# Attention with values of two pairs of heads in buffers, and the output products as two column tiles

## The reference

```python
s_win = jnp.einsum('brqhd,brwkhd->bhrqwk', qg, k_strip).astype(jnp.float32) * scale
s_win = jnp.where(col_mask[:, None, :], s_win + bias.astype(jnp.float32), NEG_INF)
s_ctx = jnp.einsum('brqhd,bchd->bhrqc', qg, k_ctx).astype(jnp.float32) * scale
s = jnp.concatenate([s_win.reshape(B, NA_HEADS, rows, GRID_W, n_win), s_ctx], axis=-1)
p = jax.nn.softmax(s, axis=-1).astype(v.dtype)
o = (jnp.einsum('bhrqwk,brwkhd->brqhd', p_win, v_strip)
     + jnp.einsum('bhrqc,bchd->brqhd', p_ctx, v_ctx))
```

## Time and profile before

| what | value |
|---|---|
| median of 3 runs | 4186.23 us (4182.61 to 4192.26) |
| profiled execution: span, the only time that the page gives of it | 4189.2 us |
| PE busy over the span | 92% |
| PEld busy | 83% |
| DVE busy | 63% |
| ACT busy | 32% |
| POOL busy | 14% |

### The profile page before, as it was taken

The page is one execution under the profiler, slowest core; times in us unless marked ns, Lnnn a source line. Parts: engine busy times, 40 slices in busy tenths (PEclk is TensorE's granted clock), DMA queues, the critical chain, the costliest instruction groups (busy, mean ns, idle before and its releaser), DMA issues. The chain is left out here.

```text
span 4189.2 us, 60711 instructions
## 1 busy us (share of the span) xinstructions
PE 3859.8 (92%) x21534; PEld 3457.5 (83%) x21534; DVE 2630.6 (63%) x5384; ACT 1359.1 (32%) x1748; POOL 594.4 (14%) x516
## 2 busy tenths in 40 slices
PE   7989999878849969799999999999979999999999
PEld 6878777656538759688888888888869999999999
DVE  1313344346553358757786877777767777788887
ACT  1113333335541131123343424242423333333332
POOL 0000000000000000022222232323212222222221
PEclk7779999999979979899999999999989999999999
DMA  4411111111133311256777685958699999999997
GB/s 172 157 60 52 53 52 40 34 46 40 48 107 107 108 63 40 78 193 210 230 239 256 211 286 181 308 168 301 191 311 357 345 345 348 330 389 346 347 346 274
DMA packets 373028, 813.75 MB, mean 194 GB/s; under 512 B 30704, under 2 KB 207600, under 8 KB 369520
## 3 DMA queue, kind: packets, MB, share of 16 engines
q1 hardware_dynamic: 299120, 542.84, 37.6%
q0 software_dynamic: 73728, 268.47, 18.7%
HBM read 681.69 MB, written 129.50 MB: 194 GB/s over the span
## 5 line engine op out<-in xcount | busy, mean ns | idle before, releaser
L85 PE MATMUL s_ps_a<-back_dense_hi,s_u_hi 128*128 128x512 f32 (+1 forms) x2048 | 715.0, 349 | 47.2 <-DVE s_u_lo L1500 31.9
L85 PE MATMUL c_ps_y<-c_wa_hi,c_v_hi 128*128 128x384 f32 x2048 | 686.6, 335 | 30.1 <-DVE c_wa_lo L1832 30.1
L86 PE MATMUL s_ps_a<-back_dense_lo,s_u_hi 128*128 128x512 f32 (+1 forms) x2048 | 697.6, 341 | 0.0
L87 PE MATMUL s_ps_a<-back_dense_hi,s_u_lo 128*128 128x512 f32 (+1 forms) x2048 | 693.7, 339 | 0.0
L86 PE MATMUL c_ps_y<-c_wa_lo,c_v_hi 128*128 128x384 f32 x2048 | 685.2, 335 | 0.0
L87 PE MATMUL c_ps_y<-c_wa_hi,c_v_lo 128*128 128x384 f32 x2048 | 685.1, 335 | 0.0
L1812 ACT ACTIVATE c_v_hi<-c_v_raw 128x1024 fp32r<-128x1024 f32 x256 | 271.7, 1061 | 657.9 <-PE c_ps_y L87 616.5
L1440 POOL DMA_INDIRECT s_row<-in_u_rows,back_expert x128 | 159.3, 1245 | 2266.4 <-DVE back_expert L1602 1823.7
L85 PEld LDWEIGHTS s_ps_a<-back_dense_hi,s_u_hi 128*128 128x128 f32 x2048 | 391.3, 191 | 96.1 <-DVE s_u_lo L1500 33.3
L1830 DVE TENSOR_TENSOR c_v_lo<-c_v_raw,c_v_hi 128x1024 fp32r<-128x1024 f32 x256 | 313.6, 1225 | 195.4 <-ACT c_v_hi L1812 179.8
L87 PEld LDWEIGHTS s_ps_a<-back_dense_hi,s_u_lo 128*128 128x128 f32 x2048 | 388.7, 190 | 46.8
(11 more groups left out here) (317 smaller groups left out, 7018.3 us busy)
## 6 DMA issues: line engine op xcount, KB each, us to landing
c_v_raw<-in_v SPq DMA_DIRECT2D x256, 512.0 KB
s_u_raw<-in_u SPq DMA_DIRECT2D x130, 512.0 KB
act_scratch<-s_a SPq DMA_DIRECT2D x128, 384.0 KB
gm_scratch<-s_gm SPq DMA_DIRECT2D x48, 1024.0 KB
c_a<-act_scratch SPq DMA_DIRECT2D x256, 192.0 KB
c_g<-gm_scratch SPq DMA_DIRECT2D x256, 192.0 KB
a_w<-in_w_ada SPq DMA_DIRECT2D x16, 1024.0 KB, 4.7
q_raw<-in_w_pq SPq DMA_DIRECT2D x17, 512.0 KB, 3.6
```

Of the source, the lines that this page charges most:

```text
L85: nc.tensor.matmul(out, w_hi, x_hi, start=first, stop=False)
L86: nc.tensor.matmul(out, w_hi, x_lo, start=False, stop=False)
L87: return nc.tensor.matmul(out, w_lo, x_hi, start=False, stop=last)
```

## The change

Three edits. The value tiles get a second buffer, with a semaphore for each; the values of pair h + 1 are issued in turn 2 of pair h, behind the store of the finished pair and the slab, after the last output products of pair h - 1. The output products are split by head: 64 value columns of the head as weights, the 64 query columns of the head as moving operand, written to that head's 64 partitions of `ps_o`, which is now 64 columns wide; the products of the two heads alternate. DVE copies `ps_o` with one instruction.

```diff
-        v = m.sb("v", [P, VT, P])
-        v_odd = m.sb("v_odd", [P, VS, P])
+        v = m.sb("v", [P, 2, VT, P])
+        v_odd = m.sb("v_odd", [P, 2, VS, P])
...
-        ps_o = ps_t[:, ALL:ALL + P]
+        ps_o = ps_t[:, ALL:ALL + HD]
...
-                if h >= 1:
-                    sp.wait_ge(o_ready, ROWS * h)
-                sp.dma_start(v[:], io["v_scr"][:, cols].rearrange("(j p) c -> p j c", p=P)).then_inc(v_in, 16)
+                if h >= 2:
+                    sp.wait_ge(o_ready, ROWS * (h - 1))
+                sp.dma_start(v[:, h % 2], io["v_scr"][:, cols].rearrange("(j p) c -> p j c", p=P)).then_inc(v_in[h % 2], 16)
...
                     if h >= 1:
-                        values_in(h)
                         sp.wait_ge(o_copied, ROWS * h)
                         sp.dma_start(io["oa_scr"][h - 1], o[:, (h - 1) % 2]).then_inc(o_stored, 16)
                     if h + 1 < PAIRS:
                         slab_load(h + 1)
+                        values_in(h + 1)
...
-                    nc.vector.tensor_copy(o[0:HD, r // ROWS % 2, cols], ps_o[0:HD, 0:HD])
-                    nc.vector.tensor_copy(o[HD:P, r // ROWS % 2, cols], ps_o[HD:P, HD:P]).then_inc(o_copied, 1)
+                    nc.vector.tensor_copy(o[:, r // ROWS % 2, cols], ps_o).then_inc(o_copied, 1)
...
                     if r % ROWS == 0:
-                        pe.wait_ge(v_in, 32 * (r // ROWS + 1))
+                        pe.wait_ge(v_in[r // ROWS % 2], 32 * (r // ROWS // 2 + 1))
...
                     for j in range(NT):
-                        v_tile = tiles[:, first // 2 + j] if j < KEYS // P else v[:, T // P + j - KEYS // P]
-                        last = nc.tensor.matmul(ps_o, v_tile, p_t[:, r % 2, j], start=(j == 0), stop=(j == NT - 1))
+                        v_tile = tiles[:, first // 2 + j] if j < KEYS // P else own[:, T // P + j - KEYS // P]
+                        for head in (slice(0, HD), slice(HD, P)):
+                            last = nc.tensor.matmul(ps_o[head], v_tile[:, head], p_t[:, r % 2, j, head], start=(j == 0), stop=(j == NT - 1))
```

More of the change, by code:

```diff
@@ L411, in attention_and_gates @@
         ps_p = m.ps("ps_p", [P, 2, HALF])
-        ps_o = ps_t[:, ALL:ALL + P]
-        consts_in, slab_in, v_in, hi_done, lo_done, piece_ready, consts, rstd_done, slab_done, s_ready, row_max, row_stat = (
-            m.cleared_sem(x, sems) for x in ("consts_in", "slab_in", "v_in", "hi_done", "lo_done", "piece_ready", "consts", "rstd_done", "slab_done",
+        ps_o = ps_t[:, ALL:ALL + HD]
+        consts_in, slab_in, hi_done, lo_done, piece_ready, consts, rstd_done, slab_done, s_ready, row_max, row_stat = (
+            m.cleared_sem(x, sems) for x in ("consts_in", "slab_in", "hi_done", "lo_done", "piece_ready", "consts", "rstd_done", "slab_done",
                                              "s_ready", "row_max", "row_stat"))
@@ L417, in attention_and_gates @@
             m.cleared_sem(x, sems) for x in ("exp_done", "p_norm", "p_ready", "t_ready", "t_copied", "o_ready", "o_copied", "o_stored"))
-        raw_in, piece_used, gate_stored = ([m.cleared_sem(f"{x}{b}", sems) for b in range(2)] for x in ("raw_in", "piece_used", "gate_stored"))
+        raw_in, piece_used, gate_stored, v_in = ([m.cleared_sem(f"{x}{b}", sems) for b in range(2)] for x in ("raw_in", "piece_used", "gate_stored", "v_in"))
         block = ctx.enter_context(nc.Block())
@@ L444, in values_in @@
                 cols = slice(h * P, (h + 1) * P)
-                if h >= 1:
-                    sp.wait_ge(o_ready, ROWS * h)
-                sp.dma_start(v[:], io["v_scr"][:, cols].rearrange("(j p) c -> p j c", p=P)).then_inc(v_in, 16)
-                sp.dma_start(v_odd[:], io["v_scr"][GRID_W:GRID_W + VS * P, cols].rearrange("(j p) c -> p j c", p=P)).then_inc(v_in, 16)
+                if h >= 2:
+                    sp.wait_ge(o_ready, ROWS * (h - 1))
+                sp.dma_start(v[:, h % 2], io["v_scr"][:, cols].rearrange("(j p) c -> p j c", p=P)).then_inc(v_in[h % 2], 16)
+                sp.dma_start(v_odd[:, h % 2], io["v_scr"][GRID_W:GRID_W + VS * P, cols].rearrange("(j p) c -> p j c", p=P)).then_inc(v_in[h % 2], 16)
             def slab_load(h):
@@ L694, in _ @@
                     if r % ROWS == 0:
-                        pe.wait_ge(v_in, 32 * (r // ROWS + 1))
+                        pe.wait_ge(v_in[r // ROWS % 2], 32 * (r // ROWS // 2 + 1))
                     pe.wait_ge(t_copied, r + 1)
                     first = row0[r % ROWS]
-                    tiles = v if first % 2 == 0 else v_odd
+                    own, odd = v[:, r // ROWS % 2], v_odd[:, r // ROWS % 2]
+                    tiles = own if first % 2 == 0 else odd
                     for j in range(NT):
-                        v_tile = tiles[:, first // 2 + j] if j < KEYS // P else v[:, T // P + j - KEYS // P]
-                        last = nc.tensor.matmul(ps_o, v_tile, p_t[:, r % 2, j], start=(j == 0), stop=(j == NT - 1))
+                        v_tile = tiles[:, first // 2 + j] if j < KEYS // P else own[:, T // P + j - KEYS // P]
+                        for head in (slice(0, HD), slice(HD, P)):
+                            last = nc.tensor.matmul(ps_o[head], v_tile[:, head], p_t[:, r % 2, j, head], start=(j == 0), stop=(j == NT - 1))
                     last.then_inc(o_ready, 1)
```

## The result

The changed kernel takes 4140.49 us (median of 4 runs, 4136.62 to 4145.12) against 4187.42 of the kernel before in the same job; the ratio is 0.9889, 95% interval 0.9875 to 0.9903. A second job gave 0.9886 (0.9868 to 0.9905). So it is faster by 47 us, where 21 were forecast: the sign was right and the size less than half of it.

The account below looks back on a forecast made before the run. The prediction took PE to bound the kernel in the attention; its terms, -24.4 + 3.6 - 0.6 = -21.4 us, gave 4164.8 us against the median of 4186.23, with a range from 4120 to 4212.

Parts of the forecast that it names:

- The values' wait: PE's three waits for values in the attention would go with the slower turns they cause: -24.4 us, bounds 18.2 and 24.4.
- The output products: 24 small pairs a turn at 58 ns, 1.39 us against 1.34, over 64 turns: +3.6 us.
- the lower end: Output products of the two heads wholly side by side: 12 x 58 = 0.70 us a turn, -41 us.
- the signs: Changed profile: two heads' records starting together; turns with a projection piece longer than about 9.1 us or shorter than 8.5.
- The switch: PE going between whole-array and half-array products and back, twice a turn: taken as nothing.
- the upper end: Full emptying of PE at each change between whole and half array: 0.27 us, twice a turn, 64 turns, +34 us.
- Rival 3: Heads' output products side by side, with full emptying at each change of array use: 4154 us, chance 0.18.
- DVE's copy: Two copies of the outputs become one, saving time only in the stage's last three rows: 3 x 0.2 = -0.6 us.
- Clock: Shorter output products would not bring PE's clock down; at worst another 1.4 us in some turns.
- the forecast: Whole program 21.4 us faster, 4164.8 us, own range 4158 to 4178, chance 0.38.
- rivals 2 and 3: Heads' output products side by side: switches free, 4120 us, chance 0.12; or with full switches, 4154 us, chance 0.18.
- a third of 4: Rival 4: values' wait returns as another wait, 5 to 24 us of gain lost, 4170 to 4189 us, chance 0.06.

Follow-up runs that it names:

- the first experiment: Values in two buffers and loaded a pair ahead, output products and the two copies as before, against the kernel before the change: 4162.37 us, ratio 0.9936.

## Why the prediction was wrong

**The values' wait, 24.4 us: right.** With that edit alone the stage's distances sum to 24.3 us less. SP's new order delayed nothing.

**The output products, +3.6 us: wrong, and this is the step that failed.** The prediction put it so: "I take half, 53.3 ns", with 4.7 ns on top, and 24 of them in a row. The price was right: 0.058 us for a pair on its half, in both orders. "In a row" was not. With the halves alternating the two heads' pairs run side by side, and the products take 12 x 58 = 0.70 us, the lower end that the text itself worked out. So a term of +3.6 us stands where -41 for the products and at most 21 for the switches belong; the tiles alone took 24.8 us off the 61 distances (1.7 of it the clock) and 2.3 off the last rows. The choice went to the value "nearest to the rows", but every row was of products over the whole array: they bear on the price of a pair and say nothing on concurrency. The prediction had named the signs, and two were met: two records of the two heads starting together (0.007 us apart), and a turn with a piece shorter than 8.5 us (8.47).

**The switch, 0: wrong too, the other way.** 0.33 us there and back, about 60% of the upper end, paid in full only in turns with a piece. In those the net is -0.64 + 0.33 = -0.31 us (8.78 to 8.47). In a turn without one the net is -0.49 (4.45 to 3.96): PE stood idle ahead of the output products anyway, which hides 0.08 of the switch, and their first weight load was uncovered before the change too, which had already cost 0.10. Over the stage: 20 turns lose 9.6 us against the first experiment, 38 lose 11.4. Rival 3, side by side with switches, was the case that came true, with too dear a switch: with 0.33 in place of 0.54 it gives 4120 + 64 x 0.33 = 4141, beside 4140.5 measured. A fit that close is luck in part, since that sum leaves out 3.3 us of clock and the 0.18 us a turn by which 20 turns did better, and the profiled stage gained 52 us where it has 45.

**DVE's copy, -0.6: right in kind, a little too large.** Only two of the three waits of the earlier trace rows are in the last rows. They fell from 0.64 to 0.42 us each, 0.4 together. The third, 0.97 us, stands in the middle of the stage and is 1.23 after.

**Clock: not as said.** Turns keep their clock, but the three with 36 pairs of 2 moving columns do not. Their distances were 16.01, 16.01 and 14.42 us before, and 14.06, 14.09 and 14.07 after, of which the tiles explain 0.3 each. The stretches show why (columns as in the earlier trace rows), before:

```profile
521.00:524.00 3.00, 3.00 (x14) 2.90 (x15) 0.15 (x1) 0.76 (x3) 0.00 (x0) 0.50 0.02 5
524.00:527.00 3.00, 3.00 (x9) 2.33 (x8) 1.59 (x2) 1.12 (x1) 0.00 (x0) 0.52 0.00 0
```

and after:

```profile
506.00:509.00 3.00, 3.00 (x19) 2.72 (x19) 1.08 (x2) 2.33 (x3) 0.00 (x0) 0.82 0.00 0
509.00:512.00 3.00, 3.00 (x9) 2.32 (x9) 0.66 (x1) 0.15 (x1) 0.00 (x0) 0.61 0.03 5
```

The clock falls in both, for less long in the second: by the trace 6.8 us at half clock there and 3.4 here, and half of the difference is the 1.6 to 1.7 us between the two turns that the tiles do not explain. That is 3.3 us of the gain that no term of the prediction holds. In every run the clock falls in all three of these turns. In most kernels each is at 14.0 to 14.5 or at 15.6 to 16.1 us, in the one with the heads in turn three times at 16.2, and in the one with whole weights 1.3 us above either level. What decides between the two stays open.

**Two slips that change nothing.** The chances below 4178 us, "the forecast, rivals 2 and 3 and a third of 4", come to 0.70 by the prediction's own figures and not 0.68. The distance of 0.214 us at half clock is right (the records behind the second start 0.213 to 0.214 apart), though the 0.58 subtracted for it is the length of the first record and not of the last.

## What to carry to other kernels

When a product over the whole array does two heads and half of its output is thrown away, split it by head on two column tiles and let the halves alternate in the instruction list; grouped by head the same products lose. Count a change from whole array to tiles and back as about 0.33 us in a list without holes, half of what twelve such products gained, so tile a stretch, not single products. And when the term rests on something that no row shows, don't let the nearest row of another kind choose the value: put the bounds side by side and ask which of them the rows can bear on at all.

## What the runs showed of the hardware

Column tiles run side by side in float32, weight loads and all. A pair of 64 weight and 64 moving columns costs its half 0.058 us, whatever the other half does, and records on different tiles start 0.007 us apart: 12 couples in 0.70 us with two halves, 12 groups of four, one every 0.056 us, with four quarters, against 0.112 for a pair on the whole array. With the products of one half all ahead of the other's, only three or four overlap. With float32 weights of 128 columns a pair takes 0.112 us at full clock and 0.214 at half, the same with 2 or 128 moving columns (with 64 it was measured at full clock alone, 0.112): about two cycles a weight column, so the load bounds a pair when the moving operand is narrower than the weights. I had not expected that pairs could start every 7 ns, nor that going to tiles and back costs 0.33 us.

The Trainium skill, TensorEngine Tiling (Array Packing), section Key Properties, says that different tiles load and multiply in parallel, and that a change of tiling mode drains the engine. On the first these runs agree (0.007 us from one tile's record to the other's). On the second they show a price that the page does not give, 0.33 us there and back, and weight loads that are no longer hidden; that it is a drain is not shown.
